# Attention values as three split passes two steps behind the scores, and new orders at two places of the dense part, in a hybrid layer stack on one core

## What is computed

```python
def causal_block_attention(q, k, v):
    ...
        s = jnp.einsum('bqhd,bkhd->bhqk', qi, k).astype(jnp.float32)
        s = jnp.where(kpos[None, :] <= qpos[:, None], s, NEG_INF)
        p = jax.nn.softmax(s, axis=-1).astype(v.dtype)
        return jnp.einsum('bhqk,bkhd->bqhd', p, v)
    ...
        return gi[..., 0:1] * o_c + gi[..., 1:2] * o_s + gi[..., 2:3] * o_w
    ...
    k_cmp = compress(k_cmp_raw, pe_k, w1_k, w2_k)
    v_cmp = compress(v_cmp_raw, pe_v, w1_v, w2_v)
        ...
        mix = jnp.concatenate([y_a, y_b, y_c, y_d], axis=-1) @ w_out[l]
        h = layer_norm(DEEPNORM_ALPHA * h + mix, ln1_g[l], ln1_b[l])
        ff = jnp.square(jax.nn.relu(h @ w_mlp1[l])) @ w_mlp2[l]
        h = layer_norm(DEEPNORM_ALPHA * h + ff, ln2_g[l], ln2_b[l])
```

## Time and profile before

| | before |
|---|---|
| median of 3 runs | 2865.5 us (2863.94 to 2869.27) |
| the profiled execution's own time | 2868.43 us |
| its span in the trace | 2866.6 us |
| mean granted TensorE clock | 0.974 of full speed |
| busy: TensorE, VectorE, ScalarE, GpSimd | 2732.7, 1797.8, 1136.9, 249.7 us |

### The profile page before, as it was taken

One profiled execution on the slowest core, in us unless ns is written; L12 is line 12 of the kernel. 1 busy time (PEld: TensorE's weight loads), 2 busy tenths in 40 slices (PEclk: granted clock), 3 DMA queues, 4 the chain that ended last, 5 costly groups with the idle time before them and its releaser, 6 DMA issues. The chain is left out here.

```text
span 2866.6 us, 37139 instructions
## 1 busy us (share of the span) xinstructions
PE 2732.7 (95%) x13986; PEld 2187.6 (76%) x13986; DVE 1797.8 (63%) x2939; ACT 1136.9 (40%) x1817; POOL 249.7 (9%) x220
## 2 busy tenths in 40 slices
PE   5999989999989999999999999899999899999997
PEld 5899856655867887888889998566568688878886
DVE  5654454454787776786855544625547877758778
ACT  3422223434355554433433222234343555543343
POOL 3221212000000000000012212210000000000000
PEclk9999988999999999999999999889999999999999
DMA  4223233102315445986621233421032254579865
GB/s 168 65 67 102 89 100 73 32 1 81 96 65 174 144 146 197 385 307 241 220 85 59 63 94 96 105 46 30 1 110 89 90 160 144 155 249 369 288 229 189
DMA packets 254360, 387.29 MB, mean 135 GB/s; under 512 B 38608, under 2 KB 126800, under 8 KB 254184
## 3 DMA queue, kind: packets, MB, share of 16 engines
q1 hardware_dynamic: 254184, 384.92, 41.3%
HBM read 288.05 MB, written 96.83 MB: 134 GB/s over the span
## 5 line engine op out<-in xcount | busy, mean ns | idle before, releaser
L2734 ACT ACTIVATE att_PT<-att_ST 128x512 f32<-128x512 f32 (+2 forms) x244 | 135.1, 555 | 337.6 <-PE att_ST L2627 203.2
L1616 PE MATMUL mix_acc<-mix_whi,x_hi 128*128 128x256 f32 (+1 forms) x640 | 185.4, 290 | 0.0
L994 PE MATMUL dense_tr<-mlp_w,mlp_a 128*128 128x512 f32 x448 | 175.3, 391 | 5.6 <-DVE mlp_w L1292 5.6
L1618 PE MATMUL mix_acc<-mix_whi,x_lo 128*128 128x256 f32 (+1 forms) x640 | 180.0, 281 | 0.0
L1617 PE MATMUL mix_acc<-mix_wlo,x_hi 128*128 128x256 f32 (+1 forms) x640 | 179.9, 281 | 0.0
L996 PE MATMUL dense_tr<-mlp_w,mlp_a 128*128 128x512 f32 x448 | 174.4, 389 | 0.0
L995 PE MATMUL dense_tr<-mlp_w,mlp_a 128*128 128x512 f32 x448 | 174.3, 389 | 0.0
L994 PE MATMUL dense_acc<-mlp_w,mlp_a 128*128 128x512 f32 x448 | 174.3, 389 | 0.0
L996 PE MATMUL dense_acc<-mlp_w,mlp_a 128*128 128x512 f32 x448 | 174.3, 389 | 0.0
L995 PE MATMUL dense_acc<-mlp_w,mlp_a 128*128 128x512 f32 x448 | 174.3, 389 | 0.0
L644 POOL TENSOR_TENSOR norm_rstd<-norm_var,norm_power 128x1 f32<-128x1 f32 x32 | 29.8, 931 | 1476.7 <-DVE norm_var L624 1476.7
(11 more groups left out here) (432 smaller groups left out, 7488.9 us busy)
## 6 DMA issues: line engine op xcount, KB each, us to landing
mlp_w_raw<-w_mlp SPq DMA_DIRECT2D x124, 512.0 KB, 5.7
blocks<-h SPq DMA_DIRECT2D x32, 1792.0 KB, 8.2
mlp_a_raw<-blocks SPq DMA_DIRECT2D x72, 512.0 KB, 4.5
mlp_raw<-w_mlp SPq DMA_DIRECT2D x66, 512.0 KB, 6.0
ahead<-w_in SPq DMA_DIRECT2D x20, 1024.0 KB, 6.5
mlp_temp<-blocks SPq DMA_DIRECT2D x38, 512.0 KB, 4.7
residual<-h SPq DMA_DIRECT2D x32, 512.0 KB, 3.8
h<-residual SPq DMA_DIRECT2D x32, 512.0 KB, 9.2
```

Source lines behind the costliest of these rows:

```text
L994: pe.matmul(out, ah, wh, start=(ch == 0 and k == 0), stop=False, skip_group_check=True)
L1616: pe.matmul(out, xh, whi[b][:, k, 0:n], start=(k == 0), stop=False)
L1618: mm = pe.matmul(out, xl, whi[b][:, k, 0:n], start=False, stop=(k == KT - 1))
L2734: act.activation(PT[0:width, n % 3, c0:512], ST[0:width, n % 2, c0:512], ACT.Exp).then_inc(s.exp_ready, 1)
```

## The change

In the attentions the values' product becomes three fp32r passes. The mla values get a low part `vm_low` in the up-projection (in memory of y that is not yet written); the nsa values get `v_low`. ScalarE copies each step's exponentials to `PT_high`, waiting for its own exponential first; VectorE makes `PT_low` in place of `PT` (`exp_lows`, one step behind); TensorE's `values` come two steps behind the scores, and `copy_sum`, `turn_sum` and `write` one step later. `key_highs` stand at steps 11 to 14. The two halves of `u` are made at steps 11 and 14, in memory that `table` had, so they wait for GpSimd's last use of `table`. The first four maxima are turned and placed between one another. In `dense` the first products by w_out start with one tile and two row blocks; in the perceptron the activations of group 1 are made behind the copy of (2, 2), and VectorE's sums of group 1 one product later. Cut to its core:

```diff
             turn_y(1)
-            pe.wait_ge(s.y_lo, 4)
-            for k in range(KT):
+            for t in range(2):
+                pe.wait_ge(s.y_lo, 2 * t + 2)
+                for k in range(2):
+                    pe.wait_ge(s.wo_lo, k + 1)
+                    for half in range(2):
+                        products(t, half, k)
+            turn_y(2)
+            for k in range(2, KT):
                 pe.wait_ge(s.wo_lo, k + 1)
                 for t in range(2):
                     for half in range(2):
                         mm = products(t, half, k)
                         if k == KT - 1:
                             mm.then_inc(s.out_ready, 1)
-                if 1 <= k < NT - 1:
+                if k < NT - 1:
...
-            y_highs(0)
             for k in range(KT):
                 if k < 2:
                     act.wait_ge(ahead.sem, rows_loaded)
                 else:
                     act.wait_ge(wo_loaded[k % 4], 16 * ((k + 2) // 4))
                 act.activation(wo_hi[:, k, :], raw_of(k), ACT.Copy).then_inc(s.wo_hi, 1)
-                if k == 0:
-                    y_highs(1)
+                if k < 2:
+                    y_highs(k)
...
-            y_lows(0)
             for k in range(KT):
                 dve.wait_ge(s.wo_hi, k + 1)
                 dve.tensor_tensor(wo_lo[:, k, :], raw_of(k), wo_hi[:, k, :].bitcast(F32), ALU.subtract).then_inc(s.wo_lo, 1)
-                if k == 0:
-                    y_lows(1)
+                if k < 2:
+                    y_lows(k)
...
                             if g == 2:
+                                activate(1, 4)
+                                activate(1, 3)
                                 square(1, 6)
                             square(g - 1, 7)
                     elif (g, i) == (0, 1):
...
                         activate(0, 3)
                     elif (g, i) == (1, 7):
                         square(0, 7)
-                        activate(1, 4)
-                        activate(1, 3)
...
+                def rests(g):
+                    gather(g)
+                    rest12(g)
+                    rest21(g)
+                    rest1(g)
                 def collect(p):
                     g, i = order[p]
                     if g >= 2:
...
                             rest1(g)
                         elif i == 5:
                             block_sums(g - 1)
-                    elif (g, i) in ((0, 1), (1, 7)):
-                        if g:
-                            block_sums(0)
-                        gather(g)
-                        rest12(g)
-                        rest21(g)
-                        rest1(g)
-                        if g:
-                            quarter22(g)
+                        elif (g, i) == (2, 2):
+                            rests(1)
+                            quarter22(1)
+                            quarter11(1)
+                    elif (g, i) == (0, 1):
+                        rests(0)
+                    elif (g, i) == (1, 7):
+                        block_sums(0)
                     if i == 6 and g != 1:
                         quarter22(g)
-                    elif i == 7:
+                    elif i == 7 and g != 1:
...
+        vm = sbr("vm", [P, NT, H, HD + 1])
+        vm_low = nc.alloc_sbuf_tensor_at(f"{tag}_vm_low", [P, NT, D], F32R, offset=y_at)[:, :, 3 * GW:4 * GW].rearrange("p t (h d) -> p t h d", h=H)
+        v = [sbr("v0", [NK, HD + 1]), sbr("v1", [P, NT, HD + 1]), sbr("v2", [P, NT, HD + 1])]
...
-                        dve.tensor_scalar(vm[:, t, :, 0:HD], pkv(t)[:, :, NOPE:NOPE + HD], rr[:, t, 1:2], None, ALU.mult).then_inc(s.v_out, 1)
+                        dve.tensor_scalar(vm[:, t, :, 0:HD], pkv(t)[:, :, NOPE:NOPE + HD], rr[:, t, 1:2], None, ALU.mult).then_inc(s.v_high, 1)
+                        dve.wait_ge(s.v_high, t + 1)
+                        if t == 0:
+                            dve.wait_ge(late.sem, late.count)
+                        dve.scalar_tensor_tensor(vm_low[:, t, :, :], pkv(t)[:, :, NOPE:NOPE + HD], rr[:, t, 1:2], vm[:, t, :, 0:HD].bitcast(F32),
+                                                 ALU.mult, ALU.subtract).then_inc(s.v_out, 1)
...
+        KEYS0 = FIRST_HALF - 5
...
+            p_at = -(-nc.sbuf_base // 32) * 32
+            PT = sb1("PT", [P, 3, 512])
+            PT_low = nc.alloc_sbuf_tensor_at(f"{tag}_PT_low", [P, 3, 512], F32R, offset=p_at)
+            PT_high = c1.enter_context(nc.sbuf_tensor(f"{tag}_PT_high", [P, 3, 512], F32R))
...
+            v_low = [c1.enter_context(nc.sbuf_tensor(f"{tag}_v_low0", [NK, HD], F32R))]
+            v_low += [nc.alloc_sbuf_tensor_at(f"{tag}_v_low{b}", [P, NT, HD], F32R, offset=kv_at + 4 * NT * HD * (b - 1)) for b in (1, 2)]
+            u_at = -(-nc.sbuf_base // 32) * 32
+            u = sb1("u", [P, 2, NG, CMP_STRIDE])
+            table = nc.alloc_sbuf_tensor_at(f"{tag}_table", [P, T], F32, offset=u_at)
...
-                        pe.wait_ge(s.exp_ready, n + 1)
+                        pe.wait_ge(s.exp_low, n + 1)
                         if n == N0:
-                            pe.wait_ge(s.v_copied, 2)
-                            pe.wait_ge(s.v0_ready, 1)
+                            pe.wait_ge(s.v_copied, 4)
+                            pe.wait_ge(s.v0_low, 1)
                         if kt == q.keys[0] and m >= 2:
                             pe.wait_ge(s.sum_copied, m - 1)
-                        pe.matmul(VT[:, m % 2, c0:512], q.values(kt), PT[0:q.width, n % 3, c0:512], start=(kt == q.keys[0]),
-                                  stop=(kt == q.keys[-1]), skip_group_check=True).then_inc(s.valued, 1)
+                        high, low = PT_high[0:q.width, n % 3, c0:512], PT_low[0:q.width, n % 3, c0:512]
+                        pe.matmul(VT[:, m % 2, c0:512], q.values(kt), high, start=(kt == q.keys[0]), stop=False, skip_group_check=True)
+                        pe.matmul(VT[0:HD, m % 2, c0:512], q.lows(kt), high, start=False, stop=False, skip_group_check=True)
+                        pe.matmul(VT[:, m % 2, c0:512], q.values(kt), low, start=False, stop=(kt == q.keys[-1]),
+                                  skip_group_check=True).then_inc(s.valued, 1)
...
                     for u_ in first_units:
                         maxima([(u_, at) for at in range(len(pieces[u_]))])
-                    for u_ in first_units:
-                        turn_maxima(u_)
+                        if u_:
+                            turn_maxima(u_ - 1)
+                    turn_maxima(first_units[-1])
                     for n in range(len(steps)):
                         for u_ in turned_before[n]:
                             turn_maxima(u_)
                         score_T(n)
-                        if n:
-                            values(n - 1)
+                        if n >= 2:
+                            values(n - 2)
                         if n == 1:
                             pe.wait_ge(s.pe_loaded, 32)
                             pe.transpose(back[:, 0:CMP_LEN], pe_in[:], ident[0:CMP_LEN, 0:CMP_LEN]).then_inc(s.pe_turned, 1)
-                        if n - 2 in ends:
-                            turn_sum(ends[n - 2])
+                        if n - 3 in ends:
+                            turn_sum(ends[n - 3])
                         for j in range(CMP_LEN):
                             if compress_at[j] == n:
                                 compress(j)
                         if n == CMP1 + 2:
                             compressed_out()
                         maxima(behind[n])
+                    values(len(steps) - 2)
                     values(len(steps) - 1)
-                    for n in (len(steps) - 2, len(steps) - 1):
+                    for n in range(len(steps) - 3, len(steps)):
...
+                        act.wait_ge(s.exp_ready, n + 1)
+                        act.activation(PT_high[0:width, n % 3, c0:512], PT[0:width, n % 3, c0:512], ACT.Copy).then_inc(s.exp_high, 1)
+                        if n - 2 in ends:
+                            copy_sum(ends[n - 2], n - 2)
+                        if KEYS0 <= n < KEYS0 + 4:
+                            key_highs(1 + (n - KEYS0) // 2, (n - KEYS0) % 2)
...
+                    def exp_lows(n):
+                        m, kt = steps[n]
+                        width, c0 = sums[m].width, sums[m].first(kt)
+                        here = PT[0:width, n % 3, c0:512]
+                        dve.wait_ge(s.exp_high, n + 1)
+                        dve.tensor_tensor(PT_low[0:width, n % 3, c0:512], here, PT_high[0:width, n % 3, c0:512].bitcast(F32),
+                                          ALU.subtract).then_inc(s.exp_low, 1)
...
+                        if n:
+                            exp_lows(n - 1)
+                        if n - 3 in ends:
+                            write(ends[n - 3])
+                        if n in (CMP0 - 4, CMP0 - 1):
```

(40 more changed lines are left out.)

42 lines of the change are left out of this document (19 added, 23 removed).

## The result

The changed kernel takes 2921.45 us (median of 4 runs, 2909.0 to 2921.92) against 2865.57 of the kernel before in the same comparison: 1.018 times as long, interval 1.015 to 1.021. The forecast was 2832, the range ended at 2856: the sign was wrong. The profiled execution spans 2920.1 us, its mean granted clock is 0.945 in place of 0.974.

A forecast was written before the change was run, and what follows sets the result against it. TensorE, busy 95%, was taken as the bound. Per layer 3 + 5 + 0.4 = 8.4 us, twice 16.8, plus 17 for the load: 34 off 2868.4 is 2834, with the median 2.9 lower 2832 us; range 2810 to 2856.

The forecast's parts named there:

- part 2: Attention steps: with the added ScalarE copies and VectorE subtractions, nsa keeps 3 us and mla 5 us per layer.
- In mla VectorE has room.: mla steps: VectorE, busy 40.1 of 115.9 us, has room for the subtractions; 5 of 6.1 us kept per layer.
- part 3: Queries' load: earlier key copies remove its wait and the clock loss; 6 us in layer 0, 11 in layer 1, 17 together.
- well before 470: mla steps, layer 0: GpSimd's two rounds of copy and subtraction on the keys end well before 470 us.
- GpSimd and the subtraction: mla stretches: each GpSimd instruction holds one subtraction for its own length; 12.8 us per layer, 25.6 in all, 2858; chance 0.05.
- the load's wait: Step 22: ScalarE waits 5.22 us in layer 0, 2.86 in layer 1; clock loss behind it priced at 3.2 and 8.0 us.
- The mla forecast of about 105 us a layer: Sign that the prediction is right: the mla steps take about 105 us, from 115.9 in the profile before.
- Part 1: Value products of 512 columns: three fp32r passes take 0.68 us instead of 0.86; saves 6.1 us mla, 13.3 nsa per layer.
- The lead: nsa sums' ends: two steps of lead take up most of 0.8 us; 0.3 us charged for each of about 15 sums.
- the slower rival: nsa sums' ends: VectorE's queue sets the pace, 2890; it decides from 0.7 us per sum; chance 0.08.
- Part 4: Small terms per layer: up-projection -1, opening +0.5, pipeline's end -1.1, dense head +1.7, perceptron +0.3; sum 0.4 us gained.
- the head: Start of the dense part: TensorE needs only tile 0 and one row block; +1.7 us per layer (1 to 2.5).

The follow-up runs named there:

- without the collision: The changed kernel with GpSimd filling the lower halves of the two key operands with zeros instead of its copy and subtraction; 2834.62 us, ratio 0.991.
- The dense part alone: The kernel before with only the new orders of the dense part and the perceptron, its attention untouched; 2858.3 us, ratio 0.999.

## Why the prediction was wrong, by its steps

**The step that failed is in part 2: "In mla VectorE has room."** It was read from the average, 40.1 of 115.9 us. The first stretch of the earlier trace rows already said 24.15 of 37.6. The change adds a subtraction to each of these steps, and VectorE is busy 29.64 of 36 and 5.59 of the next 6 us. Into that stretch part 3 moved GpSimd's two-input work, which the earlier trace rows still had in the next one. Each part was costed as if the other did not exist: part 3 asked what the early keys do to the load, and not what GpSimd meets five steps sooner. Its own "well before 470" failed by this too: GpSimd is done with the keys at 470.44.

**The rival that named the mechanism, GpSimd and the subtraction, had a chance of 0.05 and a price of 2858.** It charged GpSimd's durations, as direct waits (25.6 us for both layers), and the prediction put the clock behind such a gap at nothing, though it priced the same thing behind the load's wait. The waits that TensorE has at `PT_low` are small, 11.8 us over both layers in the whole kernel; the rest of the loss is the 92 us at 0.50 behind the gap in each layer. The rule cited from the Trainium skill (SBUF — State Buffer, Who interferes with whom) holds: 0.56 us without GpSimd's reads, 1.93 beside them, with the same tile. The blocking shows too: the subtraction that starts at 464.29 ends 0.42 us after GpSimd's at 465.80, and the one of 2.61 us ends 0.29 us after GpSimd's next at 470.44.

**The mla forecast of about 105 us a layer was right but for this:** 104.6 and 104.8 without the collision. The whole run, which leaves out the low part of the nsa keys, gave 0.991 (0.988 to 0.994) where the forecast, 2832 of 2865.5, is 0.988.

**Part 1** holds at full clock: the passes of 512 columns start at 463.59, 463.88 and 464.11, 0.29 and 0.23 us apart. In nsa the medians are 0.24, 0.23 and, to the next instruction, 0.23: 0.70 us for the three, forecast 0.68.

**Part 2, nsa:** the sum kept 3 us a layer; 4.8 and 4.9 were measured, from first scores to last and so without the pipeline's end. VectorE is the bound of the first stretch as foretold (32.43 of 35.3 us busy), and TensorE is busy 82.75 of 84 us in the middle one. The lead takes up more than I charged; the slower rival, 0.7 us per sum, is refuted.

**Part 3** has the right mechanism (load at 470.53, no wait) and a size twice too large: 17 us, 9 measured. The term is the clock loss of layer 1, 8 us: it was that of one execution. With the same attention another had 114.4 us in these steps in place of 120.6.

**Part 4:** from the last scores to the first product by w_out it takes 10.6 us in both layers in place of 11.2 and 12.0; 1.1 lost and 1.7 gained were forecast, 0.6. The dense part alone takes 9.4 in both, so that the head gives 1.8 and 2.6 by itself. The opening from the first maxima to the first scores takes 15.1 and 16.0 us in place of 14.6 and 14.6 (forecast +0.5); but layer 1's took 15.6 in the run of the dense part alone too, where it is unchanged. The gap in the perceptron's opening has moved one product, to the copy behind both squares, and is 6.9 us long where it was 4.85 (TensorE's waits: us in total, times, the longest):

```profile
PE dense_acc L978 <- ACT norm_gain L1068: 13.8, 2, 6.9
...
PE dense_tr L978 <- ACT mlp_copy L1062: 3.8, 2, 1.9
```

The accounts of the two profiles close: +57.5 us in mla, -9.7 in nsa, -2.0 from there to the first product by w_out, -2.5 from it to layer 0's second half of the perceptron, +2.6 in the up-projections, +2.0 in the openings, and +5.6 elsewhere. Of these, 2.8 stand between layer 0's perceptron and layer 1's up-projection, where nothing was changed (665.6 us became 668.4), 2.3 behind layer 1's first product by w_out, 0.5 ahead of everything. The cause of these 5.6 wasn't tried.

## What to carry to other kernels

Cost a change stage by stage with all its parts in place: work moved for one part's sake can meet the instructions that another part adds, above all two-input VectorE operations beside GpSimd reads. Where TensorE is the bound, price a gap by how long the clock stays down behind it and not by its length, and take that from several executions. Where one stretch is full and the next is empty, apply the costlier variant only in the empty one: that kept the gain here, with 0.987 in place of 1.018.

## What the runs showed of the hardware that was not expected

- In both layers the clock fell behind one wait of 1.06 us, with TensorE busy 4.62 of the 6 us from 460 to 466. It stayed at 1.00 with the same 4.62 of 6 us in layer 1's nsa steps of the same trace, 2036 to 2042. The busy share of such a stretch doesn't tell these apart.
- It can stay at 0.50 for 84 us in which TensorE is recorded busy throughout. Beside the same compression it came back within 3 to 20 us when one of TensorE's instructions a step was plain float32, and within 24 to 92 with three fp32r passes in its place. The Trainium skill (TensorE: Matmul & The Clock Gate, Part 1: The HAM clock gate) says that activity releases the throttle; in these rows a queue that is always full was not enough for it. What in the stream decides is not settled.
- Both sides of a collision grow: GpSimd's subtraction took 2.35 to 2.46 us where VectorE had little two-input work and 3.25 where it began beside `u`, and VectorE's 0.56 us became 1.93.
